# Weights in 1 MB halves through three buffers, a row ring of seven slots, and orders from newer durations

## What is computed

```python
y = rmsnorm(x)                                  # each of 3 layers
x = x + mixer(y)                                # window attention | gated conv | MoBA + MLA
q = (rmsnorm(x) @ w_query); s = q . sub_keys    # 128 x 2 scores per head
idx, g = product_top16(s)                       # 16 of 128*128 experts per head, softmax g
a = einsum('td,thkd->thk', xc, take(expert_u, idx))
w = g * gelu(a)
x = x + einsum('thk,thkd->td', w, take(expert_v, idx))
...
```

## Time and profile before

| What | Value |
|---|---|
| Median of three runs | 2382.01 us |
| The profiled execution's own time | 2380.57 us |
| Its span, first to last instruction | 2378.6 us |
| PE, DVE, ACT, POOL busy | 75%, 72%, 38%, 40% of the span |
| Moved by DMA | 945.00 MB, 397 GB/s over the span |
| Row gathers (768) | 805.36 MB, landing in 15.3 us at the median |
| Weight quarters through `wbuf` | 194 of 512 KB, landing in 12.9 us at the median |

### The profile page before, as it was taken

How to read it: one execution, slowest core, us unless ns; L and a number is a source line. 1 busy time by engine, 2 the same in 40 slices (tenths; PEclk the granted TensorE clock), 3 DMA queues, 4 the chain that set the end, 5 groups by cost and what they waited for, 6 DMA issues and landing times.

```text
span 2378.6 us, 20718 instructions
## 1 busy us (share of the span) xinstructions
PE 1772.5 (75%) x6022; PEld 918.7 (39%) x6022; DVE 1722.0 (72%) x3620; ACT 909.5 (38%) x2610; POOL 948.1 (40%) x772
## 2 busy tenths in 40 slices
PE   9887788778775067886877677887667779888776
PEld 5642435326451045642323232642233355222222
DVE  4488888878679987678886486788659768864444
ACT  3244653343133231234442552244256224443333
POOL 0134553235335554333444252254325424444342
PEclk9999889998898589999999879899988989999999
DMA  5599999999999999999999899999989999999997
GB/s 206 177 419 421 422 421 419 417 421 418 417 368 416 422 420 418 416 417 420 421 408 417 319 417 417 397 421 421 417 318 408 419 416 395 421 422 421 422 421 318
DMA packets 151816, 945.00 MB, mean 397 GB/s; under 512 B 17631, under 2 KB 17815, under 8 KB 53399
## 3 DMA queue, kind: packets, MB, share of 16 engines
q0 software_dynamic: 110592, 805.36, 82.1%
q1 hardware_dynamic: 41110, 138.33, 14.9%
HBM read 942.57 MB, written 1.05 MB: 397 GB/s over the span
## 4 chain that ended last, share of the span: by engine, by line
DMA 52%; PE 23%; DVE 13%; ACT 7%; issue 4%; POOL 1%; DVEq 0%; ACTq 0%; SPq 0%; POOLq 0%
DMA ring<-in_uv,idx 39%; DMA wbuf<-in_wts 13%; PE y L1195 10%; DVE ring L1588 5%; PE acc L1077 5%; PE acc L1070 4%; DVE x L1579 4%; POOL ring L981 1%; ACT diag L1369 1%; ACT L1356 1%; ACT wgt L1359 1%; PE y L1077 1%; PE tp L1124 1%; ACT ge L1356 1%; ACT L1316 0%
## 5 line engine op out<-in xcount | busy, mean ns | idle before, releaser
L981 POOL DMA_INDIRECT ring<-in_uv,idx x768 | 947.9, 1234 | 1402.6 <-PE y L1195 923.7
L1195 PE MATMUL y<-ring,diag 128*128 128x512 f32 x2052 | 1056.0, 652 | 399.7 <-ACT diag L1369 388.2
L1588 DVE CUSTOM_DVE_ANT_0 ring<-ring,h 128x1024 f32<-128x1024 f32 x768 | 932.4, 1221 | 372.6 <-DMA ring<-in_uv,idx 371.1
L1195 PEld LDWEIGHTS y<-ring,diag 128*128 128x128 f32 x2052 | 385.3, 203 | 1005.5 <-ACT diag L1369 645.3
L1356 ACT ACTIVATE ge<-a 128x1 f32<-128x1 f32 x768 | 155.1, 202 | 1120.2 <-DVE a L1588 1118.4
L1579 DVE SCALAR_TENSOR_TENSOR x<-ring,wgt,x 128x1024 f32<-128x1024 f32 x255 | 327.1, 1283 | 101.6 <-ACT wgt L1359 91.3
L1070 PE MATMUL acc<-fT,wbuf 128*128 128x128 f32 x1792 | 227.5, 288 | 49.9 <-DMA wbuf<-in_wts 47.6
L1070 PEld LDWEIGHTS acc<-fT,wbuf 128*128 128x128 f32 x1792 | 220.7, 202 | 68.9 <-issue 45.5
L1359 ACT ACTIVATE wgt<-ge,gate 128x1 f32<-128x1 f32 x768 | 226.2, 295 | 25.0
L1077 PE MATMUL acc<-wbuf,fT 128*128 128x512 f32 (+1 forms) x320 | 157.4, 623 | 91.3 <-DMA wbuf<-in_wts 88.5
L1369 ACT ACTIVATE diag<-id_s,wgt 128x128 f32<-128x128 f32 x513 | 205.9, 401 | 16.7
(11 more groups left out here) (163 smaller groups left out, 1194.5 us busy)
## 6 DMA issues: line engine op xcount, KB each, us to landing
wbuf<-in_wts SPq DMA_DIRECT2D x194, 512.0 KB, 12.9
wkeep<-in_wts SPq DMA_DIRECT2D x28, 512.0 KB, 17.0
ring<-in_uv,idx POOLq DMA_INDIRECT x768, 15.3
kbuf<-in_keys SPq DMA_DIRECT2D x22, 256.0 KB, 13.2
ring<-in_wts SPq DMA_DIRECT2D x8, 512.0 KB, 8.5
caches<-in_wts SPq DMA_DIRECT2D x8, 512.0 KB, 14.8
wbuf<-in_wts SPq DMA_DIRECT2D x8, 416.0 KB, 10.5
wbuf<-in_wts SPq DMA_DIRECT2D x4, 384.0 KB, 9.0
```

The source lines that it names most:

```text
L981: nc.gpsimd.indirect_dma_start(ring[:, n % RING, :], None, uv[layer(s)], bass.IndirectOffsetOnAxis(ap=idx[:, tile(s), k:k + 1], axis=0),). ...
L1195: mm = nc.tensor.matmul(y[half][:], diag[:, (d - 1) % DIAGS, :], ring[:, n % RING, D + half * BLK:D + (half + 1) * BLK], start=(k == y_end ...
L1588: ins = v.tensor_tensor_reduce(u, u, h[:, tile(s), :], 1.0, 0.0, ALU.mult, ALU.add, a[:, c:c + 1])
```

## The change

Weight blocks are loaded in halves of 1.05 MB (8 KB for a partition) and `wbuf` has three buffers of a half, so 3.1 MB where there were 2.1 MB. `ring` has 7 slots. A buffer is given back when the second part of a product that reads the half is done. The table `US` has new durations (the mean durations of the trace, by and large). The planner's wire now has two queues, `rows` and `loads`, each in order, and each moves at half speed while both have work; a load counts as landed 3.2 us behind its last byte. The list of loads is the same but for the cut into halves.

```diff
-RING = 8
+RING = 7
-QUARTER = WBLK // 4
-STREAM = 4
+PIECE = WBLK // 2
+STREAM = 3
-US = {"quarter": 1.95, "quarter_T": 2.1, "lat_part": 1.6, "small": 0.9, "branch": 0.95, "turn": 0.8, "gain": 1.8, "score": 1.2, "av": 1.8, "key": 1.0,
-      "take": 0.65, "rms": 1.6, "norm": 1.6, "sq": 1.3, "root": 0.35, "rope": 2.7, "soft": 1.7, "end": 2.2,
...
+US = {"quarter": 1.95, "quarter_T": 2.05, "lat_part": 1.6, "small": 0.9, "branch": 0.95, "turn": 0.65, "gain": 2.0,
+      "score": 1.1, "av": 1.25, "key": 1.1, "take": 0.62, "rms": 1.65, "norm": 1.8, "sq": 1.45, "root": 0.35, "rope": 2.95,
...
-def quarters(name):
+def halves(name):
     if name == "ups":
-        return [(0, 768), (768, 768), (1536, 1024)]
-    size = 832 if name == "lat" else QUARTER
-    return [(j * size, size) for j in range(4)]
+        return [(0, 1536), (1536, 1024)]
+    size = 1664 if name == "lat" else PIECE
+    return [(0, size), (size, size)]
...
-    return s, {"bra": "bra1", "brb": "brb1"}.get(name, name), j
+    return s, {"bra": "bra1", "brb": "brb1"}.get(name, name), 2 * j + 1
...
-GB = 423.0
+GB = 421.0
+LOAD = 3.2
...
+    def wire_rate():
+        return 0.5 if wire["rows"] and wire["loads"] else 1.0
...
+    def wire_moves(at):
+        rate = wire_rate()
+        for q in ("rows", "loads"):
+            if wire[q]:
+                wire[q][0][0] -= (at - wire["at"]) * rate
+        wire["at"] = at
+        for q in ("rows", "loads"):
+            if wire[q] and wire[q][0][0] < 1e-6:
+                what = wire[q].pop(0)[1]
+                place = landed if q == "rows" else done if what[0] == "x" else loaded
+                place[what] = at + (WIRE if q == "rows" else LOAD)
+                return
...
-        wbuf = sb("wbuf", [P, STREAM, QUARTER])
+        wbuf = sb("wbuf", [P, STREAM, PIECE])
...
-                    w = weights(s, name, part)
+                    w = weights(s, name, piece(name, part))
                     cols = 416 if name == "lat" else BLK
                     for i in range(2):
                         k = 2 * part + i
-                        mm = nc.tensor.matmul(bank[:, 0:cols], fT[:, t, k, :], w[:, i * cols:(i + 1) * cols],
+                        mm = nc.tensor.matmul(bank[:, 0:cols], fT[:, t, k, :], w[:, k % 4 * cols:(k % 4 + 1) * cols],
                                               start=(k == 0), stop=(k == KT - 1))
```

More of the change, by code:

```diff
@@ L352, in block @@
             what = "kept" if kept_place(layer(s), name) else "w"
-            out.extend((what, s, name, j) for j in range(len(quarters(name))))
+            out.extend((what, s, name, j) for j in range(len(halves(name))))
     for s in range(STEPS):
@@ L393, in before_load, with piece @@
     return last_use(TILES * l, name, j)
[L396 to L400, removed]
+def piece(name, part):
+    return int(name in ("uk", "uv")) if name[0] == "u" and len(name) > 1 and name[1] in "qkv" else part // 2
 def last_part(name):
@@ L445 @@
 WIRE = 2.2
+LOAD = 3.2
 def schedule():
[L451 removed]
+    done = {}
     work, ahead = opening()
@@ L456, in schedule @@
     order = {e: [] for e in ("PE", "ACT", "DVE")}
-    free = dict.fromkeys(("PE", "ACT", "DVE", "POOL", "SP"), 0.0)
+    free = dict.fromkeys(("PE", "ACT", "DVE", "POOL", "SP", "wire"), 0.0)
     rows = {"dots": 0, "gates": 0, "y": [], "adds": [], "X": 0, "gathers": 0, "loads": 0, "finals": 0}
-    table, wire = [None], [0.0]
+    table, wire = [None], {"at": 0.0, "rows": [], "loads": [], "coming": []}
     landed, slot_free, loaded = {}, {}, {}
@@ L463, in schedule, with sent, wire_next @@
     closed = {"acc": {}, "tp": {}, "sc": {}}
[L465 to L474, removed]
+    def sent(at, queue, mb, what):
+        wire["coming"].append((at, queue, 1e3 * mb / GB, what))
+        wire["coming"].sort(key=lambda x: x[0])
+    def wire_rate():
+        return 0.5 if wire["rows"] and wire["loads"] else 1.0
+    def wire_next():
+        ends = [wire["at"] + wire[q][0][0] / wire_rate() for q in ("rows", "loads") if wire[q]]
+        return min(ends + [max(wire["at"], x[0]) for x in wire["coming"][:1]], default=None)
+    def wire_moves(at):
[10 more added lines that the diff above has]
+                return
+        _, q, us, what = wire["coming"].pop(0)
+        wire[q].append([us, what])
     def bank_opened(key):
@@ L528, in ready @@
                 block = block_of(name)
[L529 to L532, removed]
+                where = loaded_for(s, block), block, piece(name, part)
+                if where not in loaded:
+                    return None
+                at = max(at, loaded[where])
             if kind == "key":
@@ L560, in candidates @@
                     yield max(at) + US["hop"], 0, ("gather", n)
+            return
+        if engine == "wire":
+            if wire_next() is not None:
+                yield wire_next(), -1, None
             return
@@ L605, in run @@
     def run(engine, start, item):
+        if engine == "wire":
+            wire_moves(start)
+            return
         if engine == "POOL":
@@ L609, in run @@
             free["POOL"] = start + 1.3
-            landed[n] = gathered(start + 1.3)
+            sent(start + 1.0, "rows", 1.0486, n)
             return
@@ L614, in run @@
             rows["loads"] += 1
[L615 to L622, removed]
+            free["SP"] = start + 0.45
+            mb = 0.5243 * halves(name)[j][1] / D if what in ("w", "kept") else \
+                {"keys": 0.33, "x": 0.524, "const": 0.7}.get(what, 0.07)
+            sent(start + 0.5, "loads", mb, ("x", s) if what == "x" else ("keys", KEYS.index((s, int(name))))
+                 if what == "keys" else (s, name, j))
             return
@@ L1030, in weights @@
                 place = kept_place(layer(s), name)
-                first, size = quarters(name)[j]
+                first, size = halves(name)[j]
                 if place:
```

33 lines of the change are left out of this document (18 added, 15 removed).

## The result

The changed kernel takes 2348.8 us (median of four runs, 2347.8 to 2349.6), the kernel before 2382.8 us beside it: a ratio of 0.9854 [0.9838, 0.9869], 34 us less. The forecast was 2358 us with a range of 2332 to 2392.

The account below looks back on a forecast made before the run. The wire (DMA) was taken as the bound, 2244.7 of 2378.6 us. Terms -20 + 0 - 6 - 2.5 + 5 = -23.5 us gave 2357.1; with the median 1.4 us higher, the forecast was 2358 us, range 2332 to 2392.

Parts of the forecast that it names:

- rival A: The forecast itself: the leaks of the two softmaxes shrink; 2335 to 2372 us, chance 0.58.
- The order: Softmax of steps 4 and 5: more rows between exps fill the wire, -20 us, bounds 0 and -31; elsewhere 0.
- Equal shares: Wire between both queues: 8 KB loads get half, four quarters take 10 us for 15; time effect 0.
- Larger pieces by rate: Weight loads: 8 KB pieces raise load-bound stretches from 417 to 422 GB/s; -6 us, bounds 0 and -12.
- Opening: Opening, 34 to 92 us: one MB more ahead lets q2's first half be read early; -2.5 us, bound 0.
- Seven slots: Gather ring: it runs dry one row, 2.48 us, sooner at leaks; two unreturned, +5 us, bounds 0 and +25.
- rival D: Slower: the seventh slot decides, dense bursts empty the ring and leak 2.48 us more each; 2398 us, chance 0.20.
- Rival B: Loads stay at a third of the wire, ACT stands for a `take`, half of the -20 goes; 2368 us, chance 0.12.
- Rival C: Nothing measurable: the filled rows lengthen the stage by as much as they fill; 2379 us, chance 0.10.

Follow-up runs that it names:

- experiment 1: Changed layout (halves, three buffers, seven slots, 8 KB pieces) with the planner, durations and 423 GB/s of the kernel before; 2350.8 us, 0.9871 of the kernel before.
- experiment 2: Layout of the kernel before (quarters, four buffers, eight slots) with the new planner and durations; 2380.1 us, 0.9988 of the kernel before.
- experiment 3: Changed kernel, same order, buffers and slots, with each half brought by two transfers of 4 KB a partition; 2382.2 us, 1.0003 of the kernel before.
- experiment 4: Changed layout with the planner of before and each half in two transfers of 4 KB a partition; 2377.5 us, 0.9974 of the kernel before.
- experiment 6: Layout of before with the new planner, giving loads a third of the wire and rows two thirds; 2379.1 us, 0.9981 of the kernel before.
- experiment 8: Changed kernel, orders planned anew: six slots with three half buffers 2366.9 us, six with four 2357.3 us, eight with two 2366.5 us.

## Why the prediction was near in the sum and wrong in its largest step

The kernels before and after and those of experiments 1 to 4 fill this table of ratios to before:

| Layout and pieces | planner of before | new planner |
|---|---|---|
| 8 slots, 2 MB of buffers, 4 KB | 1 | 0.9988 |
| 7 slots, 3 MB, 4 KB | 0.9974 | 1.0003 |
| 7 slots, 3 MB, 8 KB | 0.9871 | 0.9854 |

From the second row to the third the kernel gains 26.7 or 33.4 us; every other step from one cell to the next is within 7. The forecast's 2358 was 9 us above the measured 2348.8: some 5 us because share, order and rate together gave 31 us where the forecast had 26, and some 5 because nothing was seen of the charge for the seventh slot. The number fell into the range of rival A, but not by A's mechanism.

**The order, forecast at -20.** Between the two planners I measured -2.0 in the changed layout, -3 in the old, and +4.6 with 7 slots and 4 KB pieces (2382.2 against 2377.5). The mechanism that I costed exists: with the layout of before, more rows between exps raise the stretch from the first to the fourth exp from 167 to 289 GB/s, at 6.7 us from exp to exp where I had 6.0. But I took the room filled in two stages as time won. Experiment 6 filled them, the second nearly, and got 25.7 and 11.2 us of dips, in which POOL waits for experts, in return. While the dense part is what sets when the next step's rows may start, rows moved forward are rows that are missing later. What stays open is whether 8 KB pieces would give as much with one row between exps: both planners put more there in the changed layout.

**Equal shares, forecast at 0.** This is the step that failed, and the order's term above is its counterpart: "While the wire is full this changes who is served, not how much: 0." The share itself came as forecast, 5.19 us a half. It is true of a moment at which the wire is full. But the dips are moments at which it isn't, and in the two largest the dense part is late: ACT stands for a product, and rows stand behind ACT. A block in 10.4 us for 15 makes the product come sooner. With the order held fixed and only the pieces changed, the dips go from 47.7 to 22.0 us with the new planner and from 46.6 to 21.8 with the old (experiment 3's profiled execution took 2377.9, its median is 2382.2, so the slices account for 29 of the 33 us). So about -25 belongs here and about -2 to the planner. That a term missing on one side was near in size to one wrong on the other was luck.

**Larger pieces by rate, forecast at -6.** What is left when share and dips are set aside is "a little under full", 7.5 to 3.6 us, and 5.4 to 3.6 against experiment 3. Load-bound stretches went to 422 as forecast. The page's own measure is larger: 14.9% of 2378.6 less 14.4% of 2346.8 is some 16 us less of queue time for the same loads (2 us either way, as the shares are rounded). About -4, the right size. The Trainium skill (DMA: Bandwidth & Descriptors, Specifications) gives 512 B as the least transfer for line rate. These runs differ from it by about 1% in load-bound stretches (1250 to 1320 with 4 KB pieces at 416 to 419 GB/s, with 8 KB in the changed kernel and experiment 1 at 422); here the measurement decides.

**Opening, forecast at -2.5.** 64.8 to 61.3 us, so -3.5. Experiment 1 has 63.2, so some of it is noise or order.

**Seven slots, forecast at +5.** Slots and buffers changed together without the pieces: -6.2 us with the old planner (experiment 4 against before), +2 with the new (experiment 3 against 2). With the opening's -2.5 I had +2.5 for the pair, just above both. Alone the seventh slot is not settled. That going on to six costs 18 us (experiment 8) shows that slots are dear at this point, as rival D had it, but one slot further down. D's 2398 didn't come, and the loss wasn't hidden by the larger pieces alone: in experiments 3 and 4 the dips are as large as before, and seven slots with three buffers still cost 2 us at most.

**Rival B,** that the share doesn't change, is refuted by the 5.19 us. Experiment 3 is that rival played out, and it would have cost far more than the 10 us that I gave it: 33. The Trainium skill (DMA: Bandwidth & Descriptors, SWDGE vs HWDGE vs iDMA) calls 4096 B the preferred most for a packet; in this trace the loads' packets fell from 41110 to 23254 as pieces doubled, so 8 KB loads were not cut. **Rival C** is ruled out by the interval of the result.

What stays open: piece size changes share and rate at once, and no run here has the one without the other. The split of 25 and 4 is read from slices, not from a run of its own. Nor is the size of a piece separated from the number of transfers: wherever a piece is 4 KB, a megabyte also comes in two transfers for one. The third and the half fit pieces of 4 and 8 KB beside the rows' 8 KB.

## What to carry to other kernels

Where two queues share a full wire, look at the size of their pieces: here the shares went with it, and a share is worth time if the smaller one feeds the work that decides when the other may go on. Before you count a filled gap as won, ask what is moved into it and whether it will be missed later: in experiment 6 the late side wasn't sped up, and the gap came back elsewhere. And split a layout change from the planner's change in two runs before believing either; here one was worth nearly all and the other some 2 us. Compare the lists that come out as well, since the same planner writes another one for another layout.

## What the runs showed of the hardware that was not expected

- A queue's share of the wire went with the bytes of its pieces: 4 KB loads beside 8 KB gathers got 137 to 141 GB/s of 417 to 418, 8 KB loads 202 of 422. With every second half cut the loss lies in between (14 of 33 us).
- The same bytes in pieces of 8 KB took 14.4% of 16 engines' span for 14.9%, 16 us of queue time, of which about 4 us showed as time.
- A slot of the ring is 2.48 us of wire, and going from seven to six costs 18 us. On the page of that kernel 15 slices between opening and end stand under 415 GB/s, for 7 in the changed kernel.
